# Choosing the first expert's token rows by products with a one-hot matrix, and asking for two weight blocks earlier, in a hybrid decoder layer

## What is computed

```python
def _hier_moe(u, rgw, rgb, rew, reb, wg, wu, wd):
    x = u.reshape(n * t, d)
    g_logits = (x @ rgw + rgb).astype(jnp.float32)
    ...
    top_v, top_i = lax.top_k(e_sel, TOP_K_IN_GROUP)
    e_w = jax.nn.softmax(top_v, axis=-1) * g_w
    e_idx = g_sel[:, None] * EXPERTS_PER_GROUP + top_i
    ...
    for e in range(N_EXPERTS):
        h = jax.nn.silu(x @ wg[e]) * (x @ wu[e])
        y = y + gates[:, e:e + 1] * (h @ wd[e]).astype(jnp.float32)
```

## Time and profile before

| what | value |
|---|---|
| median of 3 runs | 952.8 us (952.13 to 953.21) |
| the profiled execution's own time | 950.39 us |
| its span | 948.6 us |
| TensorE, VectorE, ScalarE, GpSimd busy | 887.1, 388.7, 240.0, 92.8 us |
| granted TensorE clock, mean | 0.974 |
| DMA moved | 209.56 MB, mean 221 GB/s |

### The profile page before, as it was taken

The page is one execution under the profiler, slowest core; times in us unless marked ns, Lnnn a source line. Parts: engine busy times, 40 slices in busy tenths (PEclk is TensorE's granted clock), DMA queues, the critical chain, the costliest instruction groups (busy, mean ns, idle before and its releaser), DMA issues.

```text
span 948.6 us, 15778 instructions
## 1 busy us (share of the span) xinstructions
PE 887.1 (94%) x6397; PEld 471.7 (50%) x6397; DVE 388.7 (41%) x843; ACT 240.0 (25%) x609; POOL 92.8 (10%) x126
## 2 busy tenths in 40 slices
PE   6999999999999999999989977999999979989995
PEld 4455555655447566775545653443343423433442
DVE  5217355464226567455356567211121111112453
ACT  4144222230223343243222440001000000013354
POOL 1000000000006365000000001000000000002100
PEclk9999999999999999999999997999999989999998
DMA  7664444045527764243475367999999999993111
GB/s 233 236 252 156 68 155 156 1 155 179 184 87 264 253 202 149 81 153 104 149 228 203 123 234 277 400 403 399 378 411 379 390 391 406 389 336 133 48 44 46
DMA packets 70339, 209.56 MB, mean 221 GB/s; under 512 B 18633, under 2 KB 50356, under 8 KB 61692
## 3 DMA queue, kind: packets, MB, share of 16 engines
q1 hardware_dynamic: 55840, 183.40, 52.5%
q0 software_dynamic: 4736, 16.89, 5.3%
q10 hardware_dynamic: 9692, 8.26, 2.7%
HBM read 189.09 MB, written 38.26 MB: 240 GB/s over the span
## 4 chain that ended last, share of the span: by engine, by line
PE 77%; DMA 8%; DVE 8%; ACT 4%; issue 2%; SPq 2%; ACTq 0%; DVEq 0%
PE ps L2203 18%; PE ps L2208 11%; PE ps L2630 9%; PE ps L2758 6%; PE ps L2667 5%; DMA aF<-in_moe_w_up 4%; PE ps L2478 3%; DMA EXPERT<-in_moe_w_up 3%; PE ps L2626 2%; PE ps L2240 2%; PE ps L2590 2%; PE ps L2286 2%; PE ps L2214 1%; PE ps L2367 1%; PE ps L2313 1%
## 5 line engine op out<-in xcount | busy, mean ns | idle before, releaser
L2203 PE MATMUL ps<-xT,EXPERT 128*128 128x512 f32 x384 | 175.9, 602 | 0.5 <-DVE xT L1477 0.5
L2208 PE MATMUL ps<-EXPERT,xT 128*128 128x384 f32 (+1 forms) x384 | 119.7, 453 | 0.0
L2203 PEld LDWEIGHTS ps<-xT,EXPERT 128*128 128x128 f32 x384 | 70.0, 191 | 74.7 <-issue 71.3
L2208 PEld LDWEIGHTS ps<-EXPERT,xT 128*128 128x128 f32 x384 | 77.7, 236 | 21.8
L2105 DVE TENSOR_TENSOR dF<-dF,ps 64x512 f32<-64x512 f32 (+1 forms) x24 | 14.4, 601 | 157.6 <-ACT dF L1373 157.6
L2758 PE MATMUL ps<-EXPERT,xT 128*128 128x512 f32 x128 | 56.0, 594 | 1.3 <-DVE xT L2158 1.3
L2630 PE MATMUL ps<-EXPERT,wk 128*32 128x512 f32 x384 | 47.9, 644 | 7.8 <-DMA EXPERT<-in_moe_w_up 6.6
L1377 ACT ACTIVATE dF<-ps 128x256 f32<-128x256 f32 (+1 forms) x24 | 8.4, 348 | 160.0 <-PE ps L2650 160.0
L2667 PE MATMUL ps<-EXPERT,dF 128*32 128x512 f32 x384 | 45.3, 614 | 0.5 <-issue 0.5
L1654 DVE TENSOR_REDUCE small<-ps 128x2 f32<-128x256 f32 (+3 forms) x24 | 19.8, 824 | 62.8 <-PE ps L2289 62.8
L2478 PE MATMUL ps<-EXPERT 128*128 128x512 f32 x96 | 44.0, 595 | 0.9 <-ACT EXPERT L1289 0.9
(11 more groups left out here) (507 smaller groups left out, 1366.6 us busy)
## 6 DMA issues: line engine op xcount, KB each, us to landing
EXPERT<-in_moe_w_gate SPq DMA_DIRECT2D x11, 2048.0 KB, 15.9
EXPERT<-in_moe_w_up SPq DMA_DIRECT2D x11, 2048.0 KB, 20.9
EXPERT<-in_moe_w_down SPq DMA_DIRECT2D x11, 2048.0 KB, 13.6
EXPERT<-in_w_in SPq DMA_DIRECT2D x13, 1536.0 KB, 6.8
out_win_sample<-in_cache_win SPq DMA_DIRECT2D x16, 1022.0 KB
xT<-in_moe_w_gate SPq DMA_DIRECT2D x5, 2048.0 KB, 17.4
aF<-in_moe_w_up SPq DMA_DIRECT2D x5, 2048.0 KB, 24.1
samp<-in_moe_w_down SPq DMA_DIRECT2D x5, 2048.0 KB
```

Of the source, the lines that this page charges most:

```text
L2203: last = t.matmul(ps[:, u % 2, :], W_[:, c, c0:c0 + w], xT[:, c, 0:SEQ], start=(c == 0), stop=(c == DC - 1))
L2208: last = t.matmul(ps[:, u % 2, 0:w], rows_, W_[:, c, c0:c0 + w], start=(c == 0), stop=(c == DC - 1))
```

## The change

Expert 0's rows are no longer gathered from DRAM. `R0` becomes a float32 one-hot matrix of expert 0 alone, in tile PT, and TensorE multiplies `Urow` by it: for each of the 8 column groups c (the columns c, c+8, c+16 and so on of a row) five products, one for each tile, add up in PSUM to the transposed, chosen rows. The weights of such a product (what is loaded) are 128 numbers of each row that lie 8 float32 apart, and what moves is the 96 columns of the one-hot matrix. These 40 products stand in two halves of 20, with the lists of experts 1 and 2 between. The first cast is gone, and the second one stands after three more VectorE instructions. On SP, (1, down) and (2, up) are asked for without waiting for `u_st` and the gather, and (2, gate) waits for the last of the new products. ScalarE and VectorE now wait for `u_st` ahead of their first phase.

```diff
@@ buffers
-        R0 = dF_[:, 0:FIXED * T5 * 48].bitcast(BF16).rearrange(
-            "p (e m n) -> p e m n", e=FIXED, m=T5)
+        R0 = PT[:].rearrange("p a n -> p (a n)")[:, 0:T5 * 96].rearrange("p (m n) -> p m n", m=T5)
+        R12 = dF_[:, 0:(FIXED - 1) * T5 * 48].bitcast(BF16).rearrange("p (e m n) -> p e m n", e=FIXED - 1, m=T5)
@@ SP
             sp.wait_ge(filled[4], after(("wof", NT - 1, 1)))
-            sp.wait_ge(S_["u_st"], 16 * T5)
-            sp.wait_ge(xgload[0], 16)
             load(1, 2, 1)
-            load(2, 0, 2)
             sp.wait_ge(S_["rl_pe"], T5)
             load(2, 1, 2)
+            sp.wait_ge(S_["u_st"], 16 * T5)
+            sp.wait_ge(S_["mx_pe"], 1)
+            load(2, 0, 2)
             sp.wait_ge(S_["tab_rdy"], 2)
-            sp.wait_ge(S_["list_pe"], 3)
+            sp.wait_ge(S_["list_pe"], 2)
             load(2, 2, 2)
@@ GpSimd
             pool.wait_ge(S_["u_st"], 16 * T5)
-            g.indirect_dma_start(out=xg[0][0:32 * STEP_JOBS[0]], out_offset=None, in_=u2d,
-                                 in_offset=bass.IndirectOffsetOnAxis(ap=idx0[0:32 * STEP_JOBS[0], 0:1], axis=0)).then_inc(xgload[0], 16)
-            pool.wait_ge(S_["list_ok"], 2)
             for step in range(1, FIXED):
@@ ScalarE
+            act.wait_ge(S_["u_st"], 16 * T5)
             for p in range(PH):
                 silu(p)
@@ VectorE
             def fixed_places(e):
-                v.tensor_tensor(R0[:, e], early[:, 0:96].unsqueeze(1).to_broadcast([P, T5, 96]), f2(pos0[:, e], 96),
+                v.tensor_tensor(R12[:, e - 1] if e else R0, early[:, 0:96].unsqueeze(1).to_broadcast([P, T5, 96]), f2(pos0[:, e], 96),
                                 ALU.is_equal).then_inc(S_["rank_ok"], 1)
...
             seq(v.scalar_tensor_tensor(out=key, in0=cnt, scalar=float(NE), in1=krev, op0=ALU.mult, op1=ALU.add))
-            dve.wait_ge(S_["list_pe"], 1)
-            v.tensor_copy(idx0[0:96, 0:1], ps[0:96, 2, 0:1]).then_inc(S_["list_ok"], 1)
             fixed_places(2)
             seq(v.tensor_tensor(beats, key.unsqueeze(1).to_broadcast([P, NE, NE]), f2(key, NE), ALU.is_gt))
-            dve.wait_ge(S_["list_pe"], 2)
-            v.tensor_copy(idx0[0:96, 1:FIXED], ps[0:96, 1, 0:FIXED - 1]).then_inc(S_["list_ok"], 1)
             seq(v.tensor_reduce(rnk, beats, AX.X, ALU.add))
             seq(v.tensor_scalar(over, rnk, 8.5, None, ALU.is_lt))
+            dve.wait_ge(S_["list_pe"], 1)
+            v.tensor_copy(idx12[0:96], ps[0:96, 2, 0:FIXED - 1]).then_inc(S_["list_ok"], 1)
...
+            dve.wait_ge(S_["u_st"], 16 * T5)
             for p in range(PH):
                 gated(p)
@@ TensorE
-            for e in range(FIXED):
+            def select_rows(c0, c1):
+
+                for c in range(c0, c1):
+                    for p, i in enumerate(SEQ_T):
+                        r = tile_rows(i)
+                        last = t.matmul(ps[:, c // 4, (c % 4) * P:(c % 4) * P + 96],
+                                        Urow[p][0:r].rearrange("t (p c) -> t c p", c=DC)[:, c], R0[0:r, i],
+                                        start=(p == 0), stop=(p == NT))
+                return last
+
+            pe.wait_ge(S_["rank_ok"], 1)
+            pe.wait_ge(S_["u_ok"], T5)
+            select_rows(0, DC // 2)
+            for e in range(1, FIXED):
                 pe.wait_ge(S_["rank_ok"], e + 1)
                 for i in range(T5):
                     for k in range(2):
-                        last = t.matmul(ps[0:96, 2, 0:1] if e == 0 else ps[0:96, 1, e - 1:e], R0[:, e, i], partsb[:, i, k:k + 1],
+                        last = t.matmul(ps[0:96, 2, e - 1:e], R12[:, e - 1, i], partsb[:, i, k:k + 1],
                                         start=(i + k == 0), stop=(i + k == T5))
-                if e != 1:
-                    last.then_inc(S_["list_pe"], 1)
+            last.then_inc(S_["list_pe"], 1)
+            select_rows(DC // 2, DC).then_inc(S_["mx_pe"], 1)
...
-            pe.wait_ge(S_["list_ok"], 2)
-            rows(0, 32 * STEP_JOBS[0], 16)
             for p in range(PH):
                 gate_up_start(p)
```

More of the change, by code:

```diff
@@ L571, in hybrid_kernel @@
         pos0 = take(FIXED, T5)
-        idx0 = take(FIXED, dt=I32, at=kept)
+        idx12 = take(FIXED - 1, dt=I32, at=kept)
         before = take(4, 4)
@@ L1017, in _ @@
                 g.indirect_dma_start(out=xg[step % 2][0:r], out_offset=None, in_=u2d,
-                                     in_offset=bass.IndirectOffsetOnAxis(ap=idx0[0:r, step:step + 1], axis=0)
+                                     in_offset=bass.IndirectOffsetOnAxis(ap=idx12[0:r, step - 1:step], axis=0)
                                      ).then_inc(xgload[step % 2], 16)
-            pool.wait_ge(S_["list_ok"], 3)
+            pool.wait_ge(S_["list_ok"], 2)
             def gather(j, b, r, count):
@@ L2097, in _ @@
             dve.wait_ge(S_["tab_rdy"], 2)
-            dve.wait_ge(S_["list_pe"], 3)
+            dve.wait_ge(S_["list_pe"], 2)
             v.tensor_copy(idxall, ps[:, 6, 96:96 + MAXT]).then_inc(S_["list_ok"], 1)
@@ L2699, in _ @@
                     nxt = PHASES[p][0] + 1
-                    rows(nxt % 2, 32 * STEP_JOBS[nxt], 16 * (nxt // 2 + 1))
+                    rows(nxt % 2, 32 * STEP_JOBS[nxt], 16 * (nxt // 2 + nxt % 2))
                 if p:
```

## The result

| | before, on the same chip | after |
|---|---|---|
| median of 4 runs | 952.46 us (951.39 to 953.21) | 963.55 us (961.39 to 967.31) |
| the profiled execution's own time, span | 950.39, 948.6 us | 963.58, 961.7 us |
| granted clock, mean | 0.974 | 0.965 |

The change makes the kernel slower: the ratio is 1.0113, 95% interval 1.0081 to 1.0146, some 11 us (8 to 14). The forecast was 8.1 us more and 960.9 us. The two profiled spans differ by 13.1 us.

What follows compares the result with a forecast made beforehand. VectorE's chain bounds the stage's start, then PE's chain (8.6 us slack) and the block stream (4.2 us backlog). With s 12.3, PE +3.7, stream +8.1; the later gives 952.8 + 8.1 = 960.9 us, range 954.5 to 967.0.

Steps and rivals of the forecast that it cites:

- the forecast's two chains: Expert stage: PE's chain (8.6 us slack) and the weight-block stream (4.2 us backlog); the later ends it, +8.1 us.
- step 1: TensorE at the expert stage's start: 40 float32 products, 80 loads at 0.235 us each, 18.8 us.
- The lists: TensorE at the expert stage's start: ten list products fewer, 20 left, 1.5 us.
- s: Lateness of `front` at the expert stage's start, and with it each slot release: 12.3 us.
- VectorE: Its chain ahead of `front` waits for lists and products; 7.4 us late becomes 12.3, all behind shifts whole.
- SP's queue: Blocks (1, down) and (2, up) asked for early: value nothing, beyond letting the 4.2 us backlog be the only link.
- The clock: At the products: 0.50 from 570 to 582 us; loads bound by their reading pass gain little from full clock.
- The stream's link: Weight-block stream in the expert stage: ends later by s - 4.2, the least backlog, +8.1 us.
- PE's slack alone: Rival, expert stage: stream keeps running, only PE's chain is late, by s - 8.6: +3.7, 956.5 us; chance 0.14.
- Loads that grow at the low clock: Rival, new products: stepped loads take 0.33 us at clock 0.50, s 19.9, 968.5 us; chance 0.10.
- Loads that don't mind the step: Rival, new products: 0.21 us for 26 loads at clock 0.50, then 0.105; s 4.6, 953.2 us; chance 0.11.
- Early blocks that pay: Rival, stage start: products fit under VectorE's chain, s 1.9, stream ends 2.3 us earlier, 950.5 us; chance 0.07.

Runs made afterwards that it cites:

- the fills: The kernel before, gather and SP order untouched, with 18 fills of a 512-column buffer on VectorE just ahead of `front` of step 0: 970.26 us, ratio 1.0185.
- the one-block kernel: The kernel before, gather kept, with only block (1, down) asked for early, ahead of SP's two waits: 949.42 us, ratio 0.9949.
- the kernel with the lists ahead: The changed kernel with contiguous loads and 8-row products together, plus both lists put ahead of all 40 products: 957.65 us, ratio 1.0036.

## Why the prediction was right, and where it was off

The time lay in the range, and the likeliest case (the forecast's two chains) is what happened. By its own steps:

1. *The new products* (step 1) is the term that was mis-sized. The pace of 0.235 us was met: 0.238, with single loads of 331 to 335 ns. But it said "The tile of 8 rows costs as much as one of 128". A load does; a change of rows costs 0.245 us on top, and there are 16. 80 x 0.238 + 16 x 0.245 = 23.0 us (22.9 in the trace), in place of 18.8. The run with the 8-row products together took 3.3 us of that away.
2. *The lists*: 1.7 us, forecast 1.5.
3. *The start*: 0.71 us from the one-hot matrix to the first product, as before. s came out at 16.8; of the 4.5 us above the forecast some 4.1 are step 1's, 0.2 the lists' and 0.1 lie between the last load and `front`.
4. *VectorE*: the wait for the list was 11.13 us and that for the last product 6.96, forecast 7 and 5. The order of events was right: both halves' extra time shows in both.
5. *GpSimd* cost nothing: its gather for step 1 went out at 585.26 us, and nobody waited for it.
6. *SP's queue* was half right. The stores ended later: the last landed 10.9 us after its issue, and it mattered to nobody in this kernel, while with the gather it takes the whole gain. But "value nothing, beyond letting the 4.2 us of backlog be the only link" gave the early blocks no number, and they have one: with the same s the last block comes 3.1 us later when they are asked for behind the products, and one of them alone makes the old kernel 0.5% faster.
7. *The waits for the stores* cost nothing.
8. *The clock*: 0.50 throughout, and the loads with a step still took 0.238 us, near the 0.23 that a step of 4 took at full clock.

*The sum.* The stream's link was right, its 4.2 us too large: the last block came later by s less 1.1 (the fills, blocks on time) to 3.3 us (after the change: 2.3) in the seven kernels with a late start whose blocks were not late. Why no more came back isn't shown. A likely reason is the 7.7 us for a block with nothing before it, read at 527 us, ahead of the stage: after the change the quickest block of the steps 3 to 14 took 9.8 us to land, in the other six of these kernels 8.7 to 10.1, and with these in place of 7.7 the same sum gives a backlog of 1.9 to 3.2 us. This is an estimate. In the two profiles of before and after, the lateness of the blocks "up" of the steps 5 to 14 lies anywhere from 12.8 to 16.5 us, so that one profile of each can't settle it. Behind that block up to 1.7 us were won and up to 1.7 lost, by the clock. So "s - 4.2" gives 12.6 us for s = 16.8, and that the stage had 12.8 is in part luck: the stream gave back 1.9 us too little, and the clock of this one profile 1.7 us that the sum didn't have. That TensorE's waits would shrink to 4.4 us was wrong: 7.6.

*The rivals.* PE's slack alone: the fills exclude it. Loads that grow at the low clock: excluded by 0.238 us at 0.50. Loads that don't mind the step: they do not mind it much at 0.50, but this rival also counted on full clock from the 27th load, for which it showed no row, and with contiguous loads alone the clock stayed low to the end: s 14.8, not 4.6. Early blocks that pay: its mechanism is real (the one-block kernel), only not with products, whose s never fell below 7.4.

## What to carry to other kernels

A gather that waited beside a serial chain of another engine was free here, and the work put in its place, for which that chain had to wait, was not: ask first which engine's chain the removed wait lies beside. A wait in a load queue may hold nothing back but bandwidth for somebody else: moving one block ahead of it gained 0.5%, moving two, the second 1 us ahead of the last store, let that store land 9 us later, and the gather that needs it took the gain away. Whether the second block would pay if it were asked for just behind that store was not tried. And when short products stand in a row, sort them by the number of rows of their weights.

## What the hardware did that I had not expected

- Where loads of 8 and of 128 rows follow each other, the step is 0.505 us against 0.238 (0.213 with contiguous columns), at the clock of 0.50, and the next one is shorter (0.215 and 0.165); net a change costs some 0.245 us in both cases. In the kernel with the lists ahead one such change fell into full clock: 0.28 against 0.112 us.
- A float32 load whose columns lie 8 apart takes 0.238 us at the clock of 0.50, where a contiguous one takes 0.213; at full clock the contiguous one takes 0.111. The Trainium skill's Advanced Engine Details and Errata, section SBUF Cachelines, lets each access to another line of 16 bytes pay a penalty, and has nothing on the clock. The price here is 0.025 us at the clock of 0.50; at full clock it would be some 0.12, an estimate from the 0.23 us of the earlier trace rows at a step of 4.
- The last store of 512 KB took 2.9 us with no block asked for shortly before it, 4.6 and 3.8 with one block of 2 MB asked for 5.2 and 6.5 us ahead, and 9.9 to 12.0 with two, the second 1 to 2 us ahead. In the kernel with the gather, contiguous rows and one early block, the store before it, issued 0.16 us behind the block, took 9.0 us.
